# Order of TensorE's work within a pair of attention steps, with four buffers for transposed probabilities

## Chip, cores and metric

One Trainium2 chip, one of its cores. The metric is the device time of one execution in microseconds (us), lower is better. The kernel before was run three times; one further execution was recorded by the hardware profiler.

## What is computed

A decoder trunk of one layer on 2048 tokens of width 1024: RMSNorm, one input projection, two groups of attention heads side by side, an output projection with a residual, a mixture of 32 experts, and a last RMSNorm. The change is in the attention alone:

```python
# head group A: 4 heads, each with two score maps (c = 0, 1) and one v of width 128
s = einsum('bqhcd,bkhcd->bhcqk', qblk, k) * scale
p = softmax(where(causal, s, NEG), axis=-1)
a = p[:, :, 0] - lam * p[:, :, 1]
o = einsum('bhqk,bkhd->bqhd', a, v)
...
# head group B: 8 query heads on 2 key heads, window of 128, a learned sink in each softmax
s = einsum('bnqkgd,bnjkd->bnkgqj', qb, kw) * scale
p = softmax(concat([where(valid, s, NEG), sink]), axis=-1)[..., :-1]
o = einsum('bnkgqj,bnjkd->bnqkgd', p, vw)
```

## The kernel before

The program is a row of stages: input projection, attention, output projection with the router, experts. Each stage ends on every engine before the next begins. All of what follows is in `attention` (L495 to L957).

**Steps.** A row of work is 128 queries of one head of group A ("diff", up to 2048 keys) or 128 queries of all heads of group B ("window"). `ORDER` (L512) lists the rows: group A's rows by head and query block, with a window row put in now and then behind an odd block. A row is cut into steps (`STEPS`, L520): a diff row into pieces of up to 512 keys, a window row into 4 steps, one for each pair of heads. There are 232 steps, 168 diff and 64 window. All engines walk through the same list with fixed distances, and every index below is a step's number n.

**What each engine does for a step**
- TensorE, `scores(n)` (L879): six matmuls of 64 rows (two maps or heads, one in each half of the array, times three split products) and two mask matmuls where the step touches the diagonal, into `score`, three buffers. It waits on `score_free` for the exponentials of step n-3. In a step of even number the masks stand first, in an odd one last.
- VectorE: `nmax` (L860), the maximum over both maps; later, for a diff step, `prob` (L866), map 0 times its scale plus map 1 (which GpSimd has scaled at L775; window steps are scaled by GpSimd alone, L771). When a row's last step is through, it does the row's statistics (L819 to L847), from which the scales come.
- ScalarE: two exponentials (L711, c = 0 and 1), each with a read of its accumulator.
- TensorE, `turn(u)` (L918): up to four 128x128 transposes of the finished probabilities into `aT_ps`, which has one buffer; it waits on `aT_ready`, the copy of step u-1.
- ScalarE: the copy of `aT_ps` into `aT` (L728), `TURNED` buffers; it waits on `a_turned` (the transposes of u) and on `pv_done` (the product of step u-`TURNED`).
- TensorE, `times_v(u)` (L928): the products with v, accumulated in `o_ps`, one buffer.

**Outputs.** Two diff rows (even and odd query block) share one output, a window row has its own. The last step of an output is always odd, so an output opens at an even step. Once it is accumulated, ScalarE copies `o_ps` out (L749 for diff, L745 for window, `o_ready`), and the first `times_v` of the next output waits for that copy (L930). There are 48 outputs and so 47 such waits.

**Distances.** `LAG` is 6. In its slot n ScalarE does: the copy of `aT_ps` of step n-6; exponential (n, 0); if n-8 is the last step of an output, the copy of `o_ps`; exponential (n, 1). TensorE goes in pairs of steps, p even:

```python
for pair in range(0, SLOTS, 2):
    for n in (pair, pair + 1):
        if n < N:
            scores(n)
    if 0 <= pair - LAG < N:
        turn(pair - LAG)
    for u in (pair - LAG - 2, pair - LAG - 1):
        if 0 <= u < N:
            times_v(u)
    if 0 <= pair - LAG + 1 < N:
        turn(pair - LAG + 1)
```

SyncE's queue stores the outputs and loads the next heads and windows behind `o_ready` (L671 to L693).

Of the kernel before, what the change touches and what calls it, by code (L numbers as in the profile page):

```python
# [15 lines left out]
P = 128  # L16
D = 1024
# [477 lines left out]
def attention(nc, sem, qk_d, v_d, lambdas, sinks, ident, passed, masks_d, o_d, mix_d, acc_d, n2_d, slots_d, empty_d,  # L495
              w_out, wo_hi, wo_lo, wo_raw, wo_split):

    LAG = 6
    RING = 7
    BUFS = 3  # L500
    KEEP = 2
    TURNED = 3
    CHUNK = 512
    DV = 2 * HD
    CHUNKS = SEQ // CHUNK
# [23 lines left out]
    N = len(STEPS)  # L529
    ROWS = len(ORDER)  # L530
# [11 lines left out]
    CLOSES = {LAST[m]: m for m in range(ROWS) if ORDER[m][0] == "window" or ORDER[m][2] % 2 == 1}  # L542
# [2 lines left out]
    POOLED = set()  # L545
    COMBINED = [sum(n in DIFF and n not in POOLED for n in range(u + 1)) for u in range(N)]
    HALVED = [sum(n in POOLED for n in range(u + 1)) for u in range(N)]
    SLOTS = N + LAG + 4
    LAMBDA_INIT = 0.8 - 0.6 * math.exp(-0.3 * 0)
    LAMBDA_AT = 3  # L550
    assert RING > LAG > LAMBDA_AT + 1
# [1 line left out]
    with ExitStack() as ctx:  # L553
        def sb(name, shape, dt=F32):
            return ctx.enter_context(nc.sbuf_tensor(name, shape, dt))
# [6 lines left out]
        lam_prod = sb("lam_prod", [P, 2, HD])  # L562
# [13 lines left out]
        under = sb("under", [P, 2, N])  # L576
        fac = sb("fac", [P, 2, N])
        total = sb("total", [P, 2, ROWS])
        inv = sb("inv", [P, 2, ROWS])
        scale = sb("scale", [P, 2, N])  # L580
        nrow_swa = sb("nrow_swa", [P, 2, PAIRS_SWA])
        below = sb("below_swa", [P, 2, 2, PAIRS_SWA])
# [2 lines left out]
        inv_swa = sb("inv_swa", [P, 2, PAIRS_SWA])  # L585
        aT = sb("aT", [P, TURNED, CHUNK])
        o = sb("o_diff", [P, KEEP, 2, DV])
        o_swa = sb("o_swa", [P, PAIRS_SWA, P])
        zero = sb("zero2", [P, 1, D // 8])
        masks_f = prob[:, RING - 1, 0, 0:3 * P].rearrange("p (a b) -> p a b", a=3)  # L590

        score = ps("score", [P, BUFS, 2, CHUNK])
# [5 lines left out]
        lam_step = sem("p2_lam_step")  # L598
# [31 lines left out]
        with nc.Block() as block:  # L630
# [68 lines left out]
            @block.scalar  # L699
            def _(act):  # L700
                act.sem_inc(score_free, 2 * BUFS)
                act.sem_inc(aT_ready, 1)
                act.dma_start(masks_f, masks_d.rearrange("k p n -> p k n")).then_inc(const_in, 16)
                load_v(act, 0, 0)
                for n, a in enumerate(lambdas):
                    act.dma_start(lam_in[:, n, :], row_broadcast(a, HD)).then_inc(lam_loaded, 16)
                act.dma_start(sink[:, :], row_broadcast(sinks, SWA_HEADS)).then_inc(sink_in, 16)

                def exp(n, c):
                    w = STEPS[n][4]  # L710
                    act.activation(prob[:, n % RING, c, 0:w], score[:, n % BUFS, c, 0:w], ACT.Exp,  # L711
                                   bias=nmax[:, c, n:n + 1], accum_out=part[:, c, n:n + 1]).then_inc(score_free, 1)

                for n in range(SLOTS):
                    if ENDS.get(n - 1) in LONG:
                        m = ENDS[n - 1]
                        a, b = FIRST[m], LAST[m] + 1
                        act.wait_ge(stat_step, STAT_END[m] - 4)
                        if ORDER[m][0] == "window":
                            act.activation(exps[:, :, :, :], below[:, :, :, :], ACT.Exp).then_inc(fac_ready, 1)  # L720
                        else:
                            act.activation(fac[:, :, a:b], under[:, :, a:b], ACT.Exp).then_inc(fac_ready, 1)
                    u = n - LAG
                    if 0 <= u < N:
                        w = STEPS[u][4] * (2 if STEPS[u][0] == "window" else 1)
                        act.wait_ge(a_turned, u + 1 + RING)
                        act.wait_ge(pv_done, u + 1)
                        act.copy(aT[:, u % TURNED, 0:w], aT_ps[:, 0:w]).then_inc(aT_ready, 1)  # L728
                    if n < N:
                        act.wait_ge(max_ready, n + 1)  # L730
                        act.wait_ge(a_turned, max(n + 1, RING))
                        if n == RING - 1:
                            act.wait_ge(mask_ready, 1)
                        exp(n, 0)
                    if n == LAMBDA_AT:
                        act.wait_ge(lam_step, 2)
                        act.activation(lam[:, 2:4], lam[:, 0:2], ACT.Exp).then_inc(lam_step, 1)
                    if n - LAG - 2 in CLOSES:
                        m = CLOSES[n - LAG - 2]
                        act.wait_ge(pv_done, LAST[m] + 1 + TURNED)  # L740
                        if ORDER[m][0] == "window":
                            t = ORDER[m][2]
                            if t >= 1:
                                act.wait_ge(swa_stored, 16 * t)
                            act.copy(o_swa[:, :, :].rearrange("p b t -> p (b t)"), o_ps[:, :]).then_inc(o_ready, 1)  # L745
                        else:
                            if PLACE[m] >= KEEP:
                                act.wait_ge(stored[PLACE[m] % KEEP], 16 * (PLACE[m] // KEEP))
                            act.copy(o[:, PLACE[m] % KEEP, :, :].rearrange("p r d -> p (r d)"), o_ps[:, 0:2 * DV]).then_inc(o_ready, 1)  # L749
                    if n < N:  # L750
                        exp(n, 1)

            @block.gpsimd
            def _(pool):
                def split_w(n):
                    k, cols = n // WO_PARTS, slice(n % WO_PARTS * (D // WO_PARTS), (n % WO_PARTS + 1) * (D // WO_PARTS))
                    pool.wait_ge(wo_in[k % 2], 16 * (k // 2) + 16)
                    pool.tensor_copy(wo_hi[:, k, cols], wo_raw[:, k % 2, cols]).then_inc(wo_high, 1)
                    pool.wait_ge(wo_high, n + 1)
                    pool.tensor_tensor(wo_lo[:, k, cols], wo_raw[:, k % 2, cols], wo_hi[:, k, cols], ALU.subtract)\  # L760
                        .then_inc(wo_split, 1)

                pool.memset(zero[:, :, :], 0.0).then_inc(zero_ready, 1)
                pool.wait_ge(lam_step, 5)
                for u in range(N):
                    kind, _, t, _, w, m = STEPS[u]
                    pool.wait_ge(stat_step, STAT_END[m])
                    pool.sem_inc(passed, 1)
                    slot = prob[:, u % RING, :, 0:w]
                    if kind == "window":  # L770
                        pool.tensor_tensor(slot, slot, scale[:, :, u:u + 1].to_broadcast([P, 2, w]), ALU.mult).then_inc(scaled, 1)  # L771
                        if 1 <= t <= KD:
                            split_w((t - 1) * WO_PARTS + u - FIRST[m])
                        continue
                    ins = pool.tensor_scalar(slot[:, 1, :], slot[:, 1, :], scale[:, 1, u:u + 1], lam[:, 5:6], ALU.mult, ALU.mult)  # L775
                    if u not in POOLED:
                        ins.then_inc(scaled, 1)
                        continue
                    pool.tensor_scalar(slot[:, 0, :], slot[:, 0, :], scale[:, 0, u:u + 1], None, ALU.mult).then_inc(halved, 1)
                    pool.wait_ge(halved, HALVED[u])  # L780
                    pool.tensor_tensor(slot[:, 0, :], slot[:, 0, :], slot[:, 1, :], ALU.add).then_inc(scaled, 1)
# [91 lines left out]
            def _(pe):  # L873
                spin(pe, aT_ps[:, 0:P], ident[:, :], 40)
                pe.sem_inc(a_turned, RING)
                pe.sem_inc(pv_done, TURNED)
                pe.wait_ge(mask_ready, 1)
# [50 lines left out]
                def times_v(u):  # L928
# [4 lines left out]
                    if kind == "window":  # L933
                        last = w // P - 1
                        for b in range(last + 1):
                            for c in range(2):
                                at = (c * (last + 1) + b) * P
                                mm = pe.matmul(o_ps[c * HD:(c + 1) * HD, h * P:(h + 1) * P],
                                               v_swa[:, i % 2, 1 - last + b, (h // 2) * HD:(h // 2 + 1) * HD],
                                               aT[:, u % TURNED, at:at + P], start=(b == 0), stop=(b == last))  # L940
                    else:
                        for b in range(w // P):
                            mm = pe.matmul(o_ps[:, i % 2 * DV:(i % 2 + 1) * DV], aT[:, u % TURNED, b * P:(b + 1) * P], v[:, h % 2, j // P + b, :],
                                           start=(u == FIRST[m] and b == 0), stop=(u == LAST[m] and b == w // P - 1))
                    mm.then_inc(pv_done, 1)

                for pair in range(0, SLOTS, 2):
                    for n in (pair, pair + 1):
                        if n < N:
                            scores(n)  # L950
                    if 0 <= pair - LAG < N:
                        turn(pair - LAG)
                    for u in (pair - LAG - 2, pair - LAG - 1):
                        if 0 <= u < N:
                            times_v(u)
                    if 0 <= pair - LAG + 1 < N:
                        turn(pair - LAG + 1)  # L957

# [1132 lines left out]
```

## Time and profile before

| | |
|---|---|
| median of 3 runs | 2116.08 us (2115.89 to 2117.72) |
| the profiled execution | 2119.68 us |
| its span | 2117.9 us |
| TensorE matmul busy | 1996.4 us, 94% |
| VectorE, ScalarE, GpSimd busy | 1322.4, 1159.2, 841.3 us |
| mean granted clock of TensorE | 0.975 |
| attention's matmuls | from 470 to 937 us of the span |

A span is the time from the first to the last recorded instruction of that one execution. PE is TensorE's matmul, PEld its loads of weights, DVE is VectorE, ACT ScalarE, POOL GpSimd, SP SyncE. Ends of matmuls are modelled, so the starts of successive matmuls tell more than their durations.

### The profile page before, as it was taken

What the parts mean: (1) busy time and instruction counts of PE and PEld (TensorE: products, weight loads), DVE (VectorE), ACT (ScalarE), POOL (GpSimd) and SP (SyncE); (2) the same over time, 40 slices, a digit from 0 to 9 for tenths busy, and PEclk for the clock granted to TensorE, in tenths of its full rate; (3) what the DMA queues carried; (4) which work ended last, traced back from release to release, by engine and by line L of the source; (5) the groups of instructions that cost most, each with busy time, mean ns of one, the idle gap of its engine ahead of it and who ended that gap; (6) DMA issues with size and microseconds to landing.
All of it is one profiled execution on the core that took longest, in us unless ns stands there. A gap on an engine that the chain in (4) does not pass through costs nothing. (4 is left out here: it accounts for less than half of the span.)

```text
span 2117.9 us, 39918 instructions
## 1 busy us (share of the span) xinstructions
PE 1996.4 (94%) x12659; PEld 1701.8 (80%) x12660; DVE 1322.4 (62%) x2411; ACT 1159.2 (55%) x2421; POOL 841.3 (40%) x1019
## 2 busy tenths in 40 slices
PE   7999999978999999989999689999999999999997
PEld 5888888866777787877878578788888888888886
DVE  5333333328888888854655568667777768695763
ACT  4211111118888889953333268566666657584662
POOL 3322222203655635431232245344444444454433
PEclk9999999988999999989999889999999999999998
DMA  7433333347264443224444579989989988998963
GB/s 222 143 121 119 120 121 121 111 133 194 80 184 112 126 113 91 63 73 151 154 158 137 199 231 364 365 264 311 296 278 320 342 262 285 364 342 273 313 199 88
DMA packets 320867, 420.62 MB, mean 199 GB/s; under 512 B 27913, under 2 KB 231305, under 8 KB 320752
## 3 DMA queue, kind: packets, MB, share of 16 engines
q1 hardware_dynamic: 289984, 350.88, 50.6%
q0 software_dynamic: 29136, 67.89, 12.3%
q8 instruction: 54, 0.88, 0.2%
q10 hardware_dynamic: 1648, 0.59, 0.1%
q14 instruction: 45, 0.37, 0.1%
HBM read 344.35 MB, written 110.41 MB: 215 GB/s over the span
## 5 line engine op out<-in xcount | busy, mean ns | idle before, releaser
L711 ACT ACTIVATE prob<-score,nmax 128x512 f32<-128x512 f32 (+3 forms) x464 | 264.3, 579 | 29.2 <-DVE nmax L860 28.9
L60 PE MATMUL proj<-w_in_lo,n1T_hi 128*128 128x512 f32 (+1 forms) x640 | 243.6, 381 | 3.1 <-DVE w_in_lo L297 3.0
L860 DVE TENSOR_REDUCE nmax<-score 128x2 f32<-128x1024 f32 (+3 forms) x232 | 212.6, 920 | 44.5 <-PE score L908 42.8
L62 PE MATMUL proj<-w_in_hi,n1T_hi 128*128 128x512 f32 (+1 forms) x640 | 238.8, 373 | 0.0
L61 PE MATMUL proj<-w_in_hi,n1T_lo 128*128 128x512 f32 (+1 forms) x640 | 238.8, 373 | 0.0
L60 PE MATMUL u_ps<-wu_lo,xT_hi 128*128 128x256 f32 x752 | 216.3, 288 | 0.0
L61 PE MATMUL u_ps<-wu_hi,xT_lo 128*128 128x256 f32 x752 | 212.7, 283 | 0.0
L62 PE MATMUL u_ps<-wu_hi,xT_hi 128*128 128x256 f32 x752 | 212.7, 283 | 0.0
L775 POOL TENSOR_SCALAR prob<-prob,scale,lam 128x512 f32<-128x512 f32 (+3 forms) x168 | 138.8, 838 | 160.6 <-DVE scale L847 142.0
L1855 DVE TENSOR_TENSOR wg_lo<-raw_pieces,wg_hi 128x1024 fp32r<-128x1024 f32 x124 | 147.7, 1221 | 85.7 <-ACT wg_hi L1816 85.7
L316 DVE TENSOR_TENSOR cosx<-proj,rope_sb 128x512 f32<-128x512 f32 (+1 forms) x64 | 37.9, 592 | 214.2 <-PE proj L62 210.4
L60 PE MATMUL y_ps<-wd_lo,hT_hi 128*128 128x512 f32 x376 | 155.3, 413 | 10.1 <-DVE hT_lo L1866 10.1
L1855 DVE TENSOR_TENSOR wd_lo<-raw_pieces,wd_hi 128x1024 fp32r<-128x1024 f32 x128 | 148.3, 1219 | 11.8 <-ACT wd_hi L1839 11.3
L728 ACT COPY aT<-aT_ps 128x512 f32<-128x512 f32 (+3 forms) x232 | 122.4, 528 | 52.8 <-PE aT_ps L925 50.9
L925 PE MATMUL aT_ps<-ident,prob 128*128 128x128 f32 x792 | 130.9, 281 | 17.9 <-DVE prob L866 13.8
L62 PE MATMUL y_ps<-wd_hi,hT_hi 128*128 128x512 f32 x376 | 147.3, 392 | 0.0
L61 PE MATMUL y_ps<-wd_hi,hT_lo 128*128 128x512 f32 x376 | 146.8, 390 | 0.0
L60 PE MATMUL g_ps<-wg_lo,xT_hi 128*128 128x512 f32 x376 | 146.7, 390 | 0.0
L61 PE MATMUL g_ps<-wg_hi,xT_lo 128*128 128x512 f32 x376 | 146.5, 390 | 0.0
L1816 ACT CAST wu_hi<-raw_pieces 128x1024 fp32r<-128x1024 f32 x124 | 128.8, 1053 | 32.1 <-DMA raw_pieces<-in_w_up 28.2
L62 PE MATMUL g_ps<-wg_hi,xT_hi 128*128 128x512 f32 x376 | 146.3, 389 | 0.0
L1855 DVE TENSOR_TENSOR wu_lo<-raw_pieces,wu_hi 128x1024 fp32r<-128x1024 f32 x124 | 145.9, 1218 | 0.0
(254 smaller groups left out, 5212.2 us busy)
## 6 DMA issues: line engine op xcount, KB each, us to landing
raw_pieces<-in_w_down SPq DMA_DIRECT2D x64, 1024.0 KB, 11.8
raw_pieces<-in_w_gate SPq DMA_DIRECT2D x62, 1024.0 KB, 10.7
raw_pieces<-in_w_up SPq DMA_DIRECT2D x62, 1024.0 KB, 10.5
qk_scratch<-qkT SPq DMA_DIRECT2D x96, 256.0 KB, 2.6
xT_sb<-in_xT SPq DMA_DIRECT2D x16, 512.0 KB, 4.8
h<-in_x SPq DMA_DIRECT2D x16, 512.0 KB, 6.0
acc_scratch<-h SPq DMA_DIRECT2D x16, 512.0 KB, 3.0
n_scratch<-n SPq DMA_DIRECT2D x16, 512.0 KB, 5.1
```

What stands on the lines that cost most here:

```text
L60: pe.matmul(out, hi, w_lo, start=first, stop=False)
L61: pe.matmul(out, lo, w_hi, start=False, stop=False)
L62: return pe.matmul(out, hi, w_hi, start=False, stop=last)
L316: dve.tensor_tensor(cosx[:, slot, 0:heads, :], src, cos.to_broadcast([P, heads, HD]), ALU.mult)
L711: act.activation(prob[:, n % RING, c, 0:w], score[:, n % BUFS, c, 0:w], ACT.Exp, bias=nmax[:, c, n:n + 1], accum_out=part[:, c, n:n + 1]). ...
L728: act.copy(aT[:, u % TURNED, 0:w], aT_ps[:, 0:w]).then_inc(aT_ready, 1)
L775: ins = pool.tensor_scalar(slot[:, 1, :], slot[:, 1, :], scale[:, 1, u:u + 1], lam[:, 5:6], ALU.mult, ALU.mult)
L860: dve.tensor_reduce(nmax[:, :, n:n + 1], score[:, n % BUFS, :, 0:w], AX.X, ALU.max, negate=True).then_inc(max_ready, 1)
L925: mm = pe.transpose(aT_ps[:, n * P:(n + 1) * P], prob[:, u % RING, c, b * P:(b + 1) * P], ident[:, :])
L1816: act.copy(piece(HI, k), raw_piece(raw, k)).then_inc(hi_ready, 1)
L1855: dve.tensor_tensor(piece(LO, k), raw_piece(raw, k), piece(HI, k), ALU.subtract)\
```

## The change

The order in a pair becomes: scores of p, the products with v of steps p-10 and p-9, transposes of p-6, scores of p+1, transposes of p-5. The products so come one pair later than before. `aT` gets a fourth buffer (a copy into it, of p-6, now waits for the product of p-10). ScalarE's copy of `o_ps` moves two slots later, to n-10. The list of slots is two longer. To make room, the reciprocal of a row's sums is written in place, and the block of zeros that is stored once to memory reuses the tile of lambda's products; GpSimd therefore clears it after its wait for lambda.

```diff
-    TURNED = 3
+    TURNED = 4
...
-    SLOTS = N + LAG + 4
+    SLOTS = N + LAG + 6
...
-        inv = sb("inv", [P, 2, ROWS])
+        inv = total
...
-        zero = sb("zero2", [P, 1, D // 8])
+        zero = lam_prod[:, :, :].rearrange("p (o a) d -> p o (a d)", o=1)
...
-                    if n - LAG - 2 in CLOSES:
-                        m = CLOSES[n - LAG - 2]
+                    if n - LAG - 4 in CLOSES:
+                        m = CLOSES[n - LAG - 4]
...
-                pool.memset(zero[:, :, :], 0.0).then_inc(zero_ready, 1)
                 pool.wait_ge(lam_step, 5)
+                pool.sem_inc(passed, 1)
+                pool.memset(zero[:, :, :], 0.0).then_inc(zero_ready, 1)
...
                 for pair in range(0, SLOTS, 2):
-                    for n in (pair, pair + 1):
-                        if n < N:
-                            scores(n)
+                    if pair < N:
+                        scores(pair)
+                    for u in (pair - LAG - 4, pair - LAG - 3):
+                        if 0 <= u < N:
+                            times_v(u)
                     if 0 <= pair - LAG < N:
                         turn(pair - LAG)
-                    for u in (pair - LAG - 2, pair - LAG - 1):
-                        if 0 <= u < N:
-                            times_v(u)
+                    if pair + 1 < N:
+                        scores(pair + 1)
                     if 0 <= pair - LAG + 1 < N:
                         turn(pair - LAG + 1)
```

TensorE, the pair in which the window output that begins with step 42 is opened. Before, this is pair 50 (scores of steps 50 and 51, transposes of 44, products of 42 and 43, transposes of 45):

```order
L908 MATMUL score<-kT_hi,qT_lo 128x512 [waits p2_score_free]
L908 MATMUL score<-kT_hi,qT_lo 128x512
L908 MATMUL score<-kT_lo,qT_hi 128x512 x2
L908 MATMUL score<-kT_hi,qT_hi 128x512 x2
L908 MATMUL score<-kT_hi,qT_lo 128x512 [waits p2_score_free]
L908 MATMUL score<-kT_hi,qT_lo 128x512
L908 MATMUL score<-kT_lo,qT_hi 128x512 x2
L908 MATMUL score<-kT_hi,qT_hi 128x512 x2
L925 MATMUL aT_ps<-ident,prob 128x128 [waits p2_aT_ready,p2_scaled]
L925 MATMUL aT_ps<-ident,prob 128x128 x3
L938 MATMUL o_ps<-aT,v_swa 64x128 [waits p2_aT_ready,p2_o_ready]
```

Now it is pair 52 (transposes of step 45, scores of 52, products of 42 and 43, transposes of 46; line numbers are one higher):

```order
L926 MATMUL aT_ps<-ident,prob 128x128 [waits p2_aT_ready,p2_scaled]
L926 MATMUL aT_ps<-ident,prob 128x128 x3
L909 MATMUL score<-kT_hi,qT_lo 128x512 [waits p2_score_free]
L909 MATMUL score<-kT_hi,qT_lo 128x512
L909 MATMUL score<-kT_lo,qT_hi 128x512 x2
L909 MATMUL score<-kT_hi,qT_hi 128x512 x2
L939 MATMUL o_ps<-aT,v_swa 64x128 [waits p2_aT_ready,p2_o_ready]
L939 MATMUL o_ps<-aT,v_swa 64x128 x3
L939 MATMUL o_ps<-aT,v_swa 64x128 [waits p2_aT_ready]
L939 MATMUL o_ps<-aT,v_swa 64x128 x3
L926 MATMUL aT_ps<-ident,prob 128x128 [waits p2_aT_ready,p2_a_ready]
```

Before, two blocks of scores and one block of transposes stand between the last transposes of the pair ahead and the product that waits for `o_ready`; now one block of scores does.

ScalarE, around the copy of the output that step 41 closed. Before, it stands in slot 49, behind the copies of `aT_ps` of steps 42 and 43:

```order
L728 COPY aT<-aT_ps 128x512 [waits p2_pv_done,p2_a_turned]
L711 ACTIVATE prob,part<-score,nmax 128x512 [waits p2_a_turned,p2_max_ready]
L711 ACTIVATE prob,part<-score,nmax 128x512
L728 COPY aT<-aT_ps 128x512 [waits p2_pv_done,p2_a_turned]
L711 ACTIVATE prob,part<-score,nmax 128x384 [waits p2_a_turned,p2_max_ready]
L749 COPY o_diff<-o_ps 128x256 [waits p2_stored0,p2_pv_done]
L711 ACTIVATE prob,part<-score,nmax 128x384
```

Now it stands in slot 51, behind the copies of steps 44 and 45:

```order
L728 COPY aT<-aT_ps 128x512 [waits p2_pv_done,p2_a_turned]
L711 ACTIVATE prob,part<-score,nmax 128x512 [waits p2_a_turned,p2_max_ready]
L711 ACTIVATE prob,part<-score,nmax 128x512
L728 COPY aT<-aT_ps 128x512 [waits p2_pv_done,p2_a_turned]
L711 ACTIVATE prob,part<-score,nmax 128x512 [waits p2_a_turned,p2_max_ready]
L749 COPY o_diff<-o_ps 128x256 [waits p2_stored0,p2_pv_done]
L711 ACTIVATE prob,part<-score,nmax 128x512
```

Only the copy of the output moved; the copies of `aT_ps` and the exponentials stand in their old order.

## Rows read from the trace of the kernel before

**Rows 1.** The page: TensorE's busy tenths in 40 equal slices of the span.
```profile
PE   7999999978999999989999689999999999999997
```
**Rows 2.** Busy time by stretch: PE, PEld, DVE, ACT, POOL, then granted clock, DMA share, GB/s.
```profile
480.00:925.00 445.00, 427.64 (x3908) 349.38 (x3905) 385.91 (x842) 386.87 (x1249) 230.70 (x290) 0.99 0.42 114
```
**Rows 3.** Waits from 480 to 925 us: waiter <- releaser: us in total, times, longest.
```profile
DVE nmax L860 <- PE score L908: 36.8, 44, 1.9
PEld aT_ps L925 <- DVE prob L866: 23.5, 36, 1.4
...
PEld score L908 <- ACT prob L711: 8.1, 35, 0.9
...
PEld o_ps L943 <- ACT o_swa L745: 2.5, 8, 0.5
PEld aT_ps L925 <- POOL prob L771: 2.4, 9, 0.6
```
**Rows 4.** Timeline of PE, pair 34 and the start of pair 36: start, us, instruction.
```profile
534.65 0.60 PE L925 MATMUL aT_ps<-ident,prob 128*128 128x128 f32 x4
535.18 0.50 PE L908 MATMUL score<-kT_hi,qT_lo 64*128 64x512 f32 x2
...
535.75 0.39 PE L908 MATMUL score<-kT_hi,qT_hi 64*128 64x512 f32 x2
535.98 0.40 PE L908 MATMUL score<-kT_hi,qT_lo 64*128 64x512 f32 x2
...
536.44 0.39 PE L908 MATMUL score<-kT_hi,qT_hi 64*128 64x512 f32 x2
536.76 0.66 PE L925 MATMUL aT_ps<-ident,prob 128*128 128x128 f32 x4
537.25 1.73 PE L943 MATMUL o_ps<-v_sb,aT 128*128 128x128 f32 x14
538.82 0.60 PE L925 MATMUL aT_ps<-ident,prob 128*128 128x128 f32 x4
```
**Rows 5.** Timeline of ACT, slots 35 and 36.
```profile
539.46 0.59 ACT L728 COPY aT<-aT_ps 128x512 f32<-128x512 f32 x1
539.95 0.69 ACT L711 ACTIVATE prob<-score,nmax 128x512 f32<-128x512 f32 x1
...
540.63 0.68 ACT L711 ACTIVATE prob<-score,nmax 128x512 f32<-128x512 f32 x1
...
541.29 0.58 ACT L728 COPY aT<-aT_ps 128x512 f32<-128x512 f32 x1
```
**Rows 6.** Timelines: copies of a diff and a window output, and the product released.
```profile
544.35 0.37 ACT L749 COPY o_diff<-o_ps 128x256 f32<-128x256 f32 x1
...
577.85 0.59 ACT L745 COPY o_swa<-o_ps 128x512 f32<-128x512 f32 x1
...
578.49 0.38 PE L943 MATMUL o_ps<-v_sb,aT 128*128 128x128 f32 x1
```
**Rows 7.** Timelines of PE and ACT, window steps of width 256.
```profile
556.85 0.28 PE L908 MATMUL score<-k_swa_hi,q_swa_lo 64*128 64x256 f32 x2
...
557.53 0.60 PE L925 MATMUL aT_ps<-ident,prob 128*128 128x128 f32 x4
...
556.45 0.48 ACT L711 ACTIVATE prob<-score,nmax 128x256 f32<-128x256 f32 x1
...
556.91 0.48 ACT L711 ACTIVATE prob<-score,nmax 128x256 f32<-128x256 f32 x1
```
**Rows 8.** Timeline of PE, transposes and window products behind them.
```profile
569.22 0.66 PE L925 MATMUL aT_ps<-ident,prob 128*128 128x128 f32 x4
569.81 1.09 PE L938 MATMUL o_ps<-aT,v_swa 128*64 128x128 f32 x16
```
**Rows 9.** Timeline: one of TensorE's long waits for VectorE in a dense stretch.
```profile
549.98 0.65 PE L925 MATMUL aT_ps<-ident,prob 128*128 128x128 f32 x4 [1.26 <-DVE prob L866]
```
**Rows 10.** VectorE's maxima at full width from 480 to 925 us: busy, mean ns, idle before.
```profile
L860 DVE TENSOR_REDUCE nmax<-score 128x2 f32<-128x1024 f32 x108 | 131.5, 1219 | 25.0 <-PE score L908 24.5
```

More of the change, by code:

```diff
@@ L761, in split_w @@
                         .then_inc(wo_split, 1)
+                pool.wait_ge(lam_step, 5)
+                pool.sem_inc(passed, 1)
                 pool.memset(zero[:, :, :], 0.0).then_inc(zero_ready, 1)
-                pool.wait_ge(lam_step, 5)
                 for u in range(N):
```

## The prediction

> **What bounds the kernel now.** The page's slices show where the change can act: attention lies in slices 9 to 18, from 470 to 937 us, where TensorE's matmuls read 9 nearly throughout [rows 1]. Nothing outside is edited, so the rest stays, and the question is how long the 232 steps take. The stretch from 480 to 925 us, by engine, shows TensorE busy 427.6 of 445 us, ScalarE 386.9, VectorE 385.9, at a granted clock of 0.99 [rows 2]: TensorE bounds it, with two engines close behind, in a loop with it.
>
> The list of waits says what TensorE still loses there [rows 3]. Before transposes it waits 23.5 + 2.4 = 25.9 us for finished probabilities; before scores 8.1 us for exponentials; before products 2.5 us for copies of outputs. VectorE's 36.8 us of waiting for scores are time of an engine that does not bound.
>
> **Part 1, the copy of the output (slower, 47 us).** The largest term. An opening product waits for the copy that ScalarE makes in the middle of slot p-1. The distance on TensorE between the last transposes of the pair ahead and that product shrinks, while ScalarE's work up to the copy is the same and starts from transposes that now follow each other closely. I work out both sides from the start of the transposes of p-8, at full width.
>
> ScalarE: from the start of transposes to their copy 0.64 us (538.82 in [rows 4] to 539.46 in [rows 5]). Copy to exponential 0.49, exponential to exponential 0.68, exponential to the next copy 0.66 [rows 5]. Then the copy of p-7 0.49, exponential (p-1, 0) 0.68, the copy of the output 0.37, and 0.05 from a copy's end to the product (577.85 + 0.59 = 578.44, to 578.49) [rows 6]. Together 4.06 us.
>
> TensorE: transposes that follow products take 0.53 up to scores (534.65 to 535.18). A block of scores that stands alone takes 0.57 to its last group (535.18 to 535.75) and from there 0.32 to a block of another kind (536.44 to 536.76), together 0.89. Transposes that follow scores take 0.49 up to products, of which 0.11 is their last step (1.57 / 14, from product to product), so 0.38 inside; and 0.53 - 3 x 0.11 = 0.20 from there to scores: 0.58. Then 0.89 again [rows 4]. Together 2.89 us.
>
> So the product is ready 1.17 us before its copy is. With window steps an exponential takes 0.46 (556.45 to 556.91) and a block of scores about 0.79 (0.68 from 556.85 to 557.53, plus an entry of 0.11) [rows 7], and the copy of a window output 0.59 [rows 6]; ScalarE's side is then 3.6 us and TensorE's 2.6, with transposes of three blocks: 1.0 us. I did the same sum for the 45 openings within the list (the two last fall in the tail), each with its own widths; they lie between 0.6 and 1.5 us, mean 1.05, **47 us**. Queued behind the waiting product are the second product, the transposes of p-6 and the scores of p+1, so VectorE and ScalarE lose the same time. The order before checks the method: its two sides, from the start of the transposes of p-7, are 0.64 + 0.49 + 0.68 + 0.37 + 0.05 = 2.23 us and 0.53 + 0.80 + 0.78 + 0.49 = 2.60: no wait with a diff output and hardly one with a window output, as the 2.5 us say [rows 3]. Bounds: 0, if such waits stay as they are, and 70, if ScalarE comes half a microsecond late besides.
>
> **Part 2, splitting the two blocks of scores (slower, 33 us).** Back to back, the blocks cost TensorE 0.80 and 0.78 us, the second without an entry. Both blocks and both blocks of transposes, without the products, took 0.53 + 0.80 + 0.78 + 0.49 = 2.60 us; now they take 0.89 + 0.53 + 0.89 + 0.58 = 2.89, and 0.05 more where products follow scores, if these slow down as transposes do (0.38 against 0.33) [rows 4]: 0.34 us. Where window products follow, TensorE paid for entering them already (0.59 us from transposes to them against 0.49) [rows 8], and I take the same for leaving them, so 0.19 is left. 81 pairs x 0.34 + 30 x 0.19 = **33 us**. TensorE bounds this stretch, so nothing covers it. Bounds: 12 (0.11 a pair, an entry alone) and 38.
>
> **Part 3, waits before transposes (faster, 18 us).** Transposes of an even step now stand behind the products, over 1 us later against the transposes ahead of them. A wait such as the 1.26 us of [rows 9], at the first step of a row of four, would go. Transposes of an odd step keep their distance of some 3 us to the scores of p; VectorE's maximum (1.22 us, [rows 10]) and the combination must fit in, and what is late next is VectorE, whose maximum of p-1 starts later because its scores do. I take about two thirds of 25.9, **18 us**; ends 0 and 28 (with the 2.5 before products).
>
> **Part 4, small ones.** Odd transposes now follow even ones behind a single block of scores, and `aT_ps` has one buffer: from transposes to the end of their copy 0.64 + 0.59 + 0.05 = 1.28 us, against 0.53 + 0.89 = 1.42 on TensorE [rows 4, 5]. At full width nothing waits; with narrow scores of p+1 (23 pairs) 0.1 us each, **2 us**, end 10. Waits for exponentials before scores stay. The tail is one product later, behind one more copy, **1 us**, ends 0 and 2. The fourth buffer of `aT` only permits the order: no wait in [rows 3] has a copy waiting for a product. Reciprocals in place cost the same. GpSimd's clear of the zeros stands where GpSimd waited anyway, and SyncE waits for it ahead of its first store, which comes later still; SyncE's loads stand behind an `o_ready` that comes one pair later, but are for the next head or the window after the next: nothing.
>
> A rule of the Trainium skill speaks for the change here. TensorE's gaps before transposes repeat through the stretch [rows 3, 9]. "Perfetto Trace Analysis", Optimization Strategy, says that a gap which repeats on the engine that should be saturated can mean too few buffers or too little room for the next tile. By it one more buffer would take those 26 us, and the sum would be -26; by the rows what was missing was probabilities, not a buffer, and I go by the rows.
>
> **Sum.** 47 + 33 - 18 + 2 + 1 = +65 us. The profiled execution took 2119.7 us, so 2184.7; it stands 3.6 us above the median of the runs shown, which makes **2181 us**. A measurement of this kernel can tell about 0.2%, 4 us, from no change.
>
> **Rivals.**
> - *Copies of outputs come nearly in time* (12%). For it: ScalarE has 58 us of idle time in the stretch [rows 2]. Against it: a copy of `aT_ps` cannot start before its transposes, so that idle time is not ahead of the chain. At 0.2 us an opening, 9 in all: 9 + 33 - 18 + 3 = +27, 2143 us.
> - *The waits were the bound* (5%), the one that ends on the other side. The loop through VectorE and ScalarE sets the pace, the 33 us fill idle time of TensorE, the outputs are copied in time, and the waits for probabilities and outputs go with all of their 28 us: 2088 us. It decides where an opening costs under 0.6 us (28 / 47) and the split is hidden. TensorE's 427.6 of 445 us speak against it [rows 2]. The rule on buffers above would end near here.
> - *The clock falls* (6%). Gaps such as that of [rows 9] left the granted clock at 0.99 over the stretch [rows 2]. With 45 more of that size it might be 0.9 in the mean: a fifth of the time at the lower of its two levels, 1.2 GHz, in which half of the work is lost, so a tenth of 467 us, 47 on top: 2228 us. "TensorE: Matmul & The Clock Gate" of the Trainium skill, A second HAM failure mode, tells of a clock that swings between its levels where TensorE idles briefly between groups of matmuls; this trace has such gaps and does not show it.
> - *The order hardly matters* (3%). What the regrouping costs and saves cancels, each under 4 us net: 2116 us.
>
> **Numbers.** The forecast has 74%. Its own range is 2152 to 2212: openings between 0.6 and 1.5 us (27 to 68), saved waits between 8 and 28, the split at 33. The range given takes in the first rival and leaves out the others: 2140 to 2212. Faster by over 0.2%: 5%, the second rival. Within 0.2%: 3%, the last. Slower: 92%.
>
> **What the changed profile would show.** TensorE's `o_ps` (now L944 and L939) waiting for ScalarE's `o_diff` and `o_swa` some 45 times, about 1 us each, in place of 2.5 us in all. From the start of a block of scores of full width to the next block 0.89 us, and attention's matmuls ending near 1002 us instead of 937. Transposes waiting for VectorE for about 8 us. A granted clock of 0.99. The first term would be wrong if those waits were under 0.3 us each; the second if pairs without an opening took as long as before; the whole if VectorE were busy nearly throughout and waited for nobody.

## The result and the profile after

The changed kernel takes 2183.85 us (median of 4 runs, 2180.96 to 2184.31), the kernel before beside it 2116.9 us. The ratio is 1.0315, 95% interval 1.0303 to 1.0327: slower by 67 us. Predicted were 2181 us and slower.

The page after, where TensorE's slices of attention (9 to 18) fall from nearly all nines; the clock holds:

```profile
span 2179.2 us, 39919 instructions
...
PE   7999999968989889897999949899999999999997
...
PEclk9999999979999999999999979999999999999998
```

TensorE's waits in its own rows, matmuls alone, from 480 to 1010 us (waiter <- releaser: us in total, times, longest). Before, the same view had one row for products, of 1.7 us:

```profile
PE o_ps L939 <- ACT o_diff L749: 16.0, 16, 1.4
PE o_ps L944 <- ACT o_swa L745: 15.4, 16, 1.5
PE o_ps L944 <- ACT o_diff L749: 12.5, 15, 1.4
```

Those are 47 waits and 43.9 us. The rows that answer to [rows 3] are those of PEld, 480 to 985 us. They count from the end of the last weight load, so the three `o_ps` rows read 57.2 us for 45 waits that are 42.2 us in the matmuls' own rows of the same stretch, some 0.3 us more for each:

```profile
PEld o_ps L939 <- ACT o_diff L749: 20.8, 15, 1.5
PEld o_ps L944 <- ACT o_swa L745: 19.2, 15, 1.9
...
PEld o_ps L944 <- ACT o_diff L749: 17.2, 15, 1.6
PEld score L909 <- ACT prob L711: 8.5, 49, 0.3
PEld aT_ps L926 <- DVE prob L867: 7.6, 15, 1.5
...
PEld aT_ps L926 <- POOL prob L776: 0.7, 2, 0.4
...
PEld aT_ps L926 <- POOL prob L772: 0.4, 1, 0.4
```

Waits of transposes for probabilities are down from 25.9 to 8.7 us; waits of scores for exponentials are as they were. Both views of one wait are rough: the matmuls' own rows have 14.3 us for probabilities before and 4.8 us now, so neither pair is the lost time to the microsecond. A count by the starts of matmuls follows behind the experiments. The same stretch by engine, to hold against [rows 2]: VectorE and ScalarE do nearly the same work (97% and 99% of the busy time) in 505 us, at the same clock.

```profile
480.00:985.00 505.00, 458.07 (x3857) 343.05 (x3854) 375.48 (x830) 382.17 (x1237) 221.45 (x289) 0.99 0.37 100
```

The opening that the prediction worked out at full width, on TensorE: transposes of 44, scores of 51, transposes of 45, scores of 52, and the first product of the window output that step 42 opens (start, us, instruction):

```profile
578.88 0.60 PE L926 MATMUL aT_ps<-ident,prob 128*128 128x128 f32 x4
579.41 0.50 PE L909 MATMUL score<-kT_hi,qT_lo 64*128 64x512 f32 x2
...
580.31 0.66 PE L926 MATMUL aT_ps<-ident,prob 128*128 128x128 f32 x4
580.89 0.50 PE L909 MATMUL score<-kT_hi,qT_lo 64*128 64x512 f32 x2
...
582.92 1.09 PE L939 MATMUL o_ps<-aT,v_swa 128*64 128x128 f32 x16 [1.06 <-ACT o_diff L749]
```

and on ScalarE:

```profile
579.52 0.59 ACT L728 COPY aT<-aT_ps 128x512 f32<-128x512 f32 x1 [0.62 <-PE aT_ps L926]
580.00 0.69 ACT L711 ACTIVATE prob<-score,nmax 128x512 f32<-128x512 f32 x1
...
580.67 0.69 ACT L711 ACTIVATE prob<-score,nmax 128x512 f32<-128x512 f32 x1
...
581.34 0.59 ACT L728 COPY aT<-aT_ps 128x512 f32<-128x512 f32 x1
581.80 0.72 ACT L711 ACTIVATE prob<-score,nmax 128x512 f32<-128x512 f32 x1
...
582.48 0.40 ACT L749 COPY o_diff<-o_ps 128x256 f32<-128x256 f32 x1
```

From the start of the transposes, 578.88, ScalarE's copy ends at 582.88 and the product starts at 582.92: 4.04 us, where 4.06 was worked out. TensorE's own part is 0.53 + 0.90 + 0.58 + 0.90 = 2.91 (2.89 worked out). The scores at 580.89 would have been followed by products at 581.79; the wait is 1.13 us.

### The profile page after: what moved, and what is told of

It reads as the page before. It is cut to its first block and busy times, and to the rows that moved or that the text cites. A ratio compares the mean times of both kernels' runs of the same rounds, so it can differ in the third digit from the quotient of the medians.

```text
span 2179.2 us, 39919 instructions
## 1 busy us (share of the span) xinstructions
PE 2028.4 (93%) x12659; PEld 1695.7 (78%) x12660; DVE 1315.2 (60%) x2411; ACT 1156.8 (53%) x2421; POOL 831.3 (38%) x1019
## 5 line engine op out<-in xcount | busy, mean ns | idle before, releaser
L776 POOL TENSOR_SCALAR prob<-prob,scale,lam 128x512 f32<-128x512 f32 (+3 forms) x168 | 130.0, 786 | 190.4 <-DVE scale L848 190.4
L944 PE MATMUL o_ps<-v_sb,aT 128*128 128x128 f32 x1088 | 145.1, 285 | 27.9 <-ACT o_swa L745 15.4
L944 PEld LDWEIGHTS o_ps<-v_sb,aT 128*128 128x128 f32 x1088 | 129.2, 193 | 51.0 <-ACT o_swa L745 20.1
```

## The experiments

Each was timed beside the kernel before on the same chip; that kernel's medians there were 2118.8 (x1 to x4), 2116.3 (x5 to x7) and 2117.0 us (x8). Ratios are to it. Times in brackets are ratio x 2117.

**x1: the output's copy one slot earlier.**

```diff
-                    if n - LAG - 4 in CLOSES:
-                        m = CLOSES[n - LAG - 4]
+                    if n - LAG - 3 in CLOSES:
+                        m = CLOSES[n - LAG - 3]
```

> The changed kernel with ScalarE's copy of the output one slot earlier (slot n-9 in place of n-10), on TensorE nothing moved. Theory A (the opening product waits because the copy stands behind the copy of p-7 and one exponential): from the start of the transposes of p-8 the copy's end is at 0.64 + 0.49 + 0.68 + 0.37 + 0.05 = 2.2 us, ahead of the 2.89 us of TensorE, so the 45 waits of about 1 us all but go, and the time is 2184 - 44 = 2140 us (2134 to 2148). Rival B (the product waits for the single accumulator itself, whatever ScalarE's order): the waits stay, 2184. Rival C (the later copies of aT_ps give the time back at the transposes): the waits go but the time stays over 2165.

Measured: 2144.15 us, ratio 1.0114 (1.0097 to 1.0131) [2141]. The only such row left in TensorE's waits, matmuls alone, 480 to 1010 us, is the one in the tail:

```profile
PE o_ps L944 <- ACT o_swa L745: 0.7, 1, 0.7
```

PEld's waits for probabilities, 480 to 952 us:

```profile
PEld aT_ps L926 <- DVE prob L867: 16.4, 32, 1.5
```

Theory A holds, B falls: the accumulator itself is not what is late, 43 of the 67 us are the copy's place. C falls as it was put (2144 is far under 2165), but something of it is there: with the openings gone, transposes wait 9 us more for VectorE than in the change.

**x8 and x2: two more places for the same copy.** Between x1 and the change, and behind it.

```diff
 # x8: ahead of exponential (n, 0)
+                    if n - LAG - 4 in CLOSES:
+                        ...
                     if n < N:
                         act.wait_ge(max_ready, n + 1)
...
 # x2: behind exponential (n, 1)
                     if n < N:
                         exp(n, 1)
+                    if n - LAG - 4 in CLOSES:
+                        ...
```

> The changed kernel with the copy of the output ahead of the first exponential of the same slot. A third place between x1 and the change: the chain to each of 45 openings is shorter by one exponential, 24 us by their widths, so the waits of products for copies fall from 44 to about 20 us and the time from 2184 to 2160 us (2154 to 2166). Rival (the wait has a floor, such as the transposes of p-7 or the accumulator): less than half of that, over 2172 us.

> The changed kernel with the copy of the output behind the second exponential of its slot in place of between the two. Theory A: the chain to each of 45 openings gets longer by one exponential, 0.68 us at full width, 0.46 at 256, 0.58 in the mean: waits of products for copies 44 + 26 = 70 us, time 2210 us (2202 to 2216). Rival B (the copy's place does not set the wait): 2184.

Measured: x8 2162.82 us, ratio 1.0214 (1.0189 to 1.0239) [2162]; x2 2220.53 us, ratio 1.0476 (1.0458 to 1.0493) [2218]. The same view, first of x8:

```profile
PE o_ps L944 <- ACT o_swa L736: 7.0, 16, 0.8
PE o_ps L939 <- ACT o_diff L740: 6.9, 14, 0.9
PE o_ps L944 <- ACT o_diff L740: 3.6, 10, 0.7
```

then of x2:

```profile
PE o_ps L939 <- ACT o_diff L751: 23.9, 15, 2.0
PE o_ps L944 <- ACT o_swa L747: 22.2, 15, 2.1
PE o_ps L944 <- ACT o_diff L751: 18.3, 14, 2.0
```

| the copy stands | waits of products, us | time above before, by the ratio, us |
|---|---|---|
| slot n-9 (x1) | 0.7 | 24 |
| slot n-10, ahead of both exponentials (x8) | 17.5 | 45 |
| between them (the change) | 43.9 | 67 |
| behind them (x2) | 64.4 | 101 |

The waits are those of one profiled execution each (x2's, of 2225.78 us, was the longest of its four), the times are medians. TensorE's instructions and their order are the same in all four. From x1 to the change the time follows the waits (+43 for +43), and x8 lies between as expected. x2 does not: its waits are 6 us under the 70 expected, its time is above the range of 2202 to 2216 us, and from the change to x2 the time rises by 34 for 21 us of waits. At least a part of the excess of 13 us is the clock, which stood at 1.00 from 520 to 820 us in the change:

```profile
520.00:820.00 300.00, 273.38 (x2334) 205.07 (x2333) 226.21 (x491) 228.73 (x734) 146.62 (x197) 1.00 0.41 113
```

and in x2 did not; three stretches of x2 (granted clock is the last but two):

```profile
520.00:820.00 300.00, 261.38 (x2149) 196.72 (x2149) 204.52 (x458) 209.84 (x680) 138.52 (x188) 0.96 0.38 104
...
560.00:580.00 20.00, 16.91 (x154) 12.64 (x153) 12.77 (x28) 13.57 (x44) 7.29 (x9) 1.00 0.51 139
580.00:600.00 20.00, 18.27 (x145) 13.23 (x144) 13.60 (x25) 14.78 (x41) 11.69 (x16) 0.91 0.12 40
```

Against 1.00 in the change's 300 us, 0.96 stands for 8% of the time at the lower level, 1.2 GHz. From 490 to 1005 us the clock is 0.96 in x2 and 1.00 in the change; an estimate from that is 0.04 x 515 = 20 us at most, enough for the whole excess. Just behind one opening at which TensorE had idled 1.73 us, the 16 window products take 1.77 us in place of the 1.09 that they take throughout the change and behind the next opening of x2:

```profile
593.39 1.77 PE L939 MATMUL o_ps<-aT,v_swa 128*64 128x128 f32 x16 [1.73 <-ACT o_diff L751]
...
598.88 1.09 PE L939 MATMUL o_ps<-aT,v_swa 128*64 128x128 f32 x16
```

So the third rival of the prediction, the falling clock, is real in x2 and all but absent in the change. It is no sharp border. Between 490 and 1005 us x2's clock fell eleven times, each time beside a wait of 1.6 to 2.1 us, but nine more waits of 1.7 to 2.0 us passed without a fall. In the change it fell once, at the longest wait of all, 1.5 us at 961.8 us (0.89 from 955 to 970 us), and in the kernel before once too, early in the attention (0.91 from 490 to 510 us).

**x3: only the split.** A small bf16 matmul between the two blocks of scores of the kernel before, output overwritten.

```diff
+                    if n % 2 == 1:
+                        pe.matmul(score[:, n % BUFS, 0, 0:P], masks[:, 0, :], masks[:, 1, :], start=True, stop=True)
                     if first:
                         mask(True, False)
```

> The kernel before with one mask matmul of 128 columns put in front of the scores of each odd step; its output is overwritten. It splits the two blocks of scores as the change does, with TensorE's order else as before. Theory A (TensorE bounds the stretch and pays for leaving and entering the 64-row form, 0.32 + 0.20 + 0.10 - 0.23 = 0.39 us less what a small bf16 matmul saves, 0.34): 116 x 0.34 = 39 us, 2156 us (2148 to 2162). Rival D (the split is hidden in TensorE's waits, only a loop through VectorE and ScalarE counts): at most the matmul's own 0.056 x 116 = 6 us, 2117 to 2124.

Measured: 2135.84 us, ratio 1.0083 (1.0066 to 1.01), +18 us. It lies between the two ranges and in neither. TensorE's own side is as predicted; its timeline of the same pair as [rows 4]:

```profile
534.79 0.60 PE L927 MATMUL aT_ps<-ident,prob 128*128 128x128 f32 x4
535.32 0.50 PE L910 MATMUL score<-kT_hi,qT_lo 64*128 64x512 f32 x2
...
536.22 0.23 PE L903 MATMUL score<-masks 128*128 128x128 bf16 x1
536.38 0.50 PE L910 MATMUL score<-kT_hi,qT_lo 64*128 64x512 f32 x2
...
537.27 0.66 PE L927 MATMUL aT_ps<-ident,prob 128*128 128x128 f32 x4
```

Scores to scores 1.06 us (0.80 before), second scores to transposes 0.89 (0.78): 0.37 us a pair with the matmul added, 43 us over 116 pairs at full width. But its PEld waits for probabilities, 480 to 942 us, are down to 7.8 us from 25.9:

```profile
PEld aT_ps L927 <- DVE prob L866: 6.7, 15, 1.0
...
PEld aT_ps L927 <- POOL prob L771: 1.1, 3, 0.4
```

A slower TensorE finds VectorE in time. 18 us by these rows come back as waits that go, without any product or transpose moved (waits of scores for exponentials rise a little, from 8.1 to 11.7 us in the rows of PEld).

**x4: buffers and shared tiles alone.**

```diff
-    TURNED = 3
+    TURNED = 4
...
-        inv = sb("inv", [P, 2, ROWS])
+        inv = total
```

(with the zeros in lambda's tile, as in the change)

> The kernel before with the change's four aT buffers, the reciprocal in place and the zeros in lambda's tile, and nothing else. Theory A: no copy into aT waits for a product before, so nothing moves: 2117 us within 4. Rival E (buffers or the shared tiles move something): more than 4 us off either way; the rule that a repeated gap means too few buffers would have up to 26 us less.

Measured: 2116.31 us, ratio 0.999 (0.9981 to 1.0): no difference above 0.2%. PEld's first row of waits is as before. The Trainium skill says of repeated gaps that they can mean too few buffers ("Perfetto Trace Analysis", Optimization Strategy); here they did not mean this buffer:

```profile
PEld aT_ps L926 <- DVE prob L867: 24.7, 37, 1.5
```

**x5, x6, x7: looking for a version better than both.** x5 is the kernel before with the copy of the output ahead of both exponentials (the edit of x8, at n-8). x6 moves one product ahead of the even transposes besides and leaves the scores together; x7 does so only where that product is of full width.

```diff
+                    if 0 <= pair - LAG - 2 < N:
+                        times_v(pair - LAG - 2)
                     if 0 <= pair - LAG < N:
                         turn(pair - LAG)
-                    for u in (pair - LAG - 2, pair - LAG - 1):
-                        if 0 <= u < N:
-                            times_v(u)
+                    if 0 <= pair - LAG - 1 < N:
+                        times_v(pair - LAG - 1)
```

> The kernel before with ScalarE's copy of the output ahead of the first exponential of its slot in place of between the two. Theory A (the copy's place sets when an opening product may start): the 3.7 us of products waiting for copies go, 2 to 4 us less; the first exponential comes 0.3 to 0.6 us later in 48 slots, which ScalarE's waits cover. 2113 to 2118 us beside 2117 of before. Rival: exponentials later by that much make scores and maxima late, over 2120.

> x5 and one product moved: scores p, scores p+1, product p-8, transposes p-6, product p-7, transposes p-5; the scores stay unsplit, three buffers as before. Even transposes stand 0.9 us later at full width, so of their 13 to 17 us of waits for probabilities 10 go. The single aT_ps buffer asks 0.64 + 0.59 + 0.15 = 1.38 us from even to odd transposes; with a full product between them TensorE takes 1.38, with narrow or window products 0.95 to 1.1, so some 55 pairs wait 0.3 us more, 16 us. Theory A: 2117 - 3 - 10 + 16 = 2120 us (2112 to 2126). Rival (only the probabilities count): 2104.

> x6 only where the product p-7 is of full width (512 keys), elsewhere the order of before. The waits for aT_ps of x6 stay away and most of the gain on even transposes at rows of full width remains, 8 us. Theory A: 2117 - 3 - 8 = 2106 us (2100 to 2113), faster than both kernels. Rival (waits for probabilities come back at the next transposes, since VectorE is late there too): 2114 to 2118.

Measured: x5 2116.83 us, ratio 0.9999 (0.9988 to 1.001), no change: in its matmuls' own rows products wait 0.9 us for copies in place of 1.7, and transposes 16.7 us for VectorE in place of 13.8. x6 2137.75 us, ratio 1.009 (1.0071 to 1.0109), 17 us above its expectation and outside its range. x7 2118.45 us, ratio 1.0008 (0.9996 to 1.002), no change, close to what its rival had and outside the range of its theory. In x6, waits of matmuls alone, 480 to 955 us, show the single buffer of `aT_ps` as expected (16 us expected):

```profile
PE aT_ps L925 <- ACT aT L728: 14.3, 48, 0.5
```

and PEld's, 480 to 1000 us, something that I had left out: scores now wait for exponentials, 20.4 us against 8.1. That later transposes make ScalarE's copies and with them its exponentials late would explain it; no run tests it.

```profile
PEld score L908 <- ACT prob L711: 20.4, 91, 0.9
PEld aT_ps L925 <- DVE prob L866: 11.7, 23, 1.2
```

The gain on transposes was there (11.7 in place of 23.5), and was more than given back. By the starts of matmuls (the count is explained below) transposes lose 22 us to the copy of `aT_ps`, products and transposes that alternate cost TensorE 9 us by themselves, which I had at nothing, and blocks of scores are 4 us longer. x7 saves no wait (23.6) and has 12.9 us before scores. No version here beats the kernel before.

**A count by the starts of matmuls.** To put the waits of the traces on one footing, I take the time from each matmul's start in the attention to the next one's and compare it with nearly the shortest (the fifth percentile) that the same neighbours take in the ten traces. A longer time in front of a transpose is put down to the probabilities or to the copy of `aT_ps`, whichever ended less than 0.2 us before it. In us:

| | before | x3 | x1 | change |
|---|---|---|---|---|
| products late for the copy of the output | 3.7 | 1.9 | 0.7 | 46.9 |
| even transposes late for probabilities | 12.0 | 1.7 | 4.3 | 0.8 |
| odd transposes late for probabilities | 7.5 | 1.7 | 7.7 | 4.7 |
| odd transposes late for the copy of `aT_ps` | 0.6 | 0.5 | 4.5 | 4.7 |
| TensorE's own steps, scores included, above before | 0 | 38 | 35 | 35 |

The rows add up to the longer attention of x3, x1 and the change (16, 26 and 66 us) within 4 us.

## Why the prediction was right

*Part 1, 47 us.* Right in mechanism and size: 47 waits (the two of the tail included), 43.9 us in all, and x1 removes them with 43 us of time. The full-width case came within 0.04 us. My ScalarE side took each engine's steps from rows where it ran without a pause, and that is how it ran.

*Part 2, 33 us.* TensorE's price was right (0.90 us from scores to another kind, 0.37 us a pair in x3 with the matmul added; 35 us in the count by starts). Wrong was "TensorE bounds this stretch, so nothing covers it". By itself the split costs 18 us (x3, with the small matmul), since it takes most of the waits for probabilities with it.

*Part 3, 18 us saved.* The size was about right: 17 us by the rows of PEld (25.9 to 8.7), 14 us by starts. The reason, even transposes standing later, is at best a part. For it: even transposes lose nearly all of their lateness in the change (12.0 to 0.8 us), and in x1, without the openings' waits, odd ones keep theirs (7.5 and 7.7) while even ones fall to 4.3. Against it: the split alone does as much in x3, where no transpose has moved (19.5 to 3.4 for both kinds). The parts are not independent. The split would have taken these waits by itself, the new order gives 8 to 9 us of them back (x1 beside x3), and the openings then hide half of that (12.0 to 5.5). Which share is whose was not separated. Parts 2 and 3 together, 15 us by the prediction, are 18 by x3. I charged the split in full and credited its saving to another cause; that the two came out alike is luck in the reasoning, and part of why the sum was within 3 us.

*Part 4.* The wait for `aT_ps` was undersized. A copy's end to the next transposes is 0.15 us, not 0.05. In the change's trace transposes start at 556.98 and 558.40 with a narrow step between, the copy ending at 557.67 + 0.58 = 558.25:

```profile
557.67 0.58 ACT L728 COPY aT<-aT_ps 128x512 f32<-128x512 f32 x1 [1.09 <-PE aT_ps L926]
```

With 0.1 us more, narrow pairs wait 0.15 to 0.25 us; by starts it is 36 waits and 4.7 us in all, where 2 were predicted. x1 stands 24 us above before, 6 more than x3, and that is what is left for the regrouping as such: 4 us more of this wait and 8 to 9 us more of waits for VectorE, less the small matmul that x3 adds; the tail was not measured by itself. The buffers and shared tiles at nothing: right (x4).

*Rivals.* "Copies come nearly in time" falls with the 43.9 us. "The waits were the bound" falls for the change, though x3 shows it half true for the split. The clock stayed at 1.00 but for one short fall; x2 shows it one exponential further on. For x2's excess over its waits (13 us) the clock is a cause seen in the rows, with at most 20 us to give, and its exact share was not separated.

## What to carry to other kernels

When an in-order engine's step is moved, work out both sides of every wait between the same two events: here the waiting engine's side shrank to 2.9 us while the releasing engine's stayed 4.1, and one copy in the wrong slot cost 43 us that an earlier slot gave back. Prices on a bounding engine and waits of that engine for its neighbours are not to be added up as if apart: slowing it by some 40 us made nearly half of that disappear from its waits (x3). Before blaming a buffer for a wait, look at who ends it: here it was VectorE, which fills the probabilities, and a buffer more changed nothing (x4).

## What was new about the hardware

- Switching between the 64-row form of the scores and 128-row matmuls costs TensorE 0.09 us on each side (0.32 to the next block where scores to scores is 0.23; 0.20 after transposes where transposes to products is 0.11) and about 0.10 us within the first group (0.33 against 0.23). It is the form and not the data type: from the kernel before, two bf16 masks of 128 rows and 128 columns are followed by f32 transposes after 0.12 us, half of the 0.22 us that two masks of 256 columns take (532.31 to 532.53), so nothing is added there, while the 64-row group ahead of the masks takes 0.21 us where the same kind of group takes 0.11 between scores:

```profile
540.21 0.28 PE L908 MATMUL score<-kT_lo,qT_hi 64*128 64x128 f32 x2
540.32 0.27 PE L908 MATMUL score<-kT_hi,qT_hi 64*128 64x128 f32 x2
540.53 0.28 PE L899 MATMUL score<-masks 128*128 128x128 bf16 x2
540.65 0.61 PE L925 MATMUL aT_ps<-ident,prob 128*128 128x128 f32 x4
```

  "TensorEngine Tiling (Array Packing)" of the Trainium skill, Key Properties, says that changing the tiling mode drains TensorE. The rows agree in that each such change costs time, and give the price, some 0.3 us for one split of two blocks; a drain itself is not seen in them.
- TensorE's granted clock fell to its lower level beside eleven single waits of 1.6 to 2.1 us in x2 (0.96 in the mean of 300 us), and once, at a wait of 1.5 us, among the 47 waits of the change (1.00 in the mean of 490 to 1005 us).
- A product starts 0.04 to 0.05 us after the copy of the output that it waits for; transposes start 0.15 us after the copy that they wait for.
